# Broadcasting 1/rms over the partitions with a diagonal split into two rounded parts

## What is computed

```python
def layer_norm(x, g, b):
    xf = x.astype(jnp.float32)
    mu = jnp.mean(xf, axis=-1, keepdims=True)
    var = jnp.mean(jnp.square(xf - mu), axis=-1, keepdims=True)
    return ((xf - mu) * lax.rsqrt(var + LN_EPS) * g + b).astype(x.dtype)

def rms_norm_2(x, g):
    xf = x.astype(jnp.float32)
    y = xf * lax.rsqrt(jnp.mean(xf * xf, axis=-1, keepdims=True) + EPS)
    return (y * g.astype(jnp.float32)).astype(x.dtype)
...
    m = rms_norm_2(mem, mem_norm_g)
    for layer in range(DEPTH):
        hn = rms_norm_2(h, mix_norm_g[layer])
        ...
        h = h + memory_cross_attention(rms_norm_2(h, xa_norm_g[layer]), m, ...)
        h = h + conv_ffn(rms_norm_2(h, ffn_norm_g[layer]), ...)
```

## Time and profile before

| | |
|---|---|
| median of 3 runs | 990.91 us (990.75 to 991.11) |
| profiled execution, first to last instruction | 989.2 us |
| VectorE busy | 686.6 us (69%) |
| ScalarE busy | 556.1 us (56%) |
| GpSimd busy | 209.3 us (21%) |
| HBM read | 166.81 MB |

### The profile page before, as it was taken

How to read it: one execution, slowest core, us unless ns; L and a number is a source line. 1 busy time by engine, 2 the same in 40 slices (tenths; PEclk the granted TensorE clock), 3 DMA queues, 4 the chain that set the end, 5 groups by cost and what they waited for, 6 DMA issues and landing times.

```text
span 989.2 us, 16695 instructions
## 1 busy us (share of the span) xinstructions
PE 972.1 (98%) x6532; PEld 879.3 (89%) x6532; DVE 686.6 (69%) x1056; ACT 556.1 (56%) x856; POOL 209.3 (21%) x199
## 2 busy tenths in 40 slices
PE   9999989999999999999999999999999999999997
PEld 8779759989988988798899899999898989989985
DVE  5789785854666687665556779776687665767973
ACT  5556673665765474555355466555445555546662
POOL 0002034300344440012003005221044301202610
PEclk9999999999999999999999999999999999999999
DMA  9634425465334447246414655457546432555441
GB/s 363 241 132 166 175 87 208 162 221 214 128 128 141 174 133 271 108 171 213 150 64 170 213 186 187 181 194 281 186 170 255 163 135 93 198 183 181 172 152 43
DMA packets 24831, 172.93 MB, mean 175 GB/s; under 512 B 2752, under 2 KB 2880, under 8 KB 4416
## 3 DMA queue, kind: packets, MB, share of 16 engines
q1 hardware_dynamic: 23040, 160.66, 45.6%
q10 hardware_dynamic: 1728, 11.40, 3.0%
HBM read 166.81 MB, written 5.24 MB: 174 GB/s over the span
## 4 chain that ended last, share of the span: by engine, by line
PE 93%; DVE 2%; ACT 2%; DMA 1%; issue 1%; POOL 0%; SPq 0%; ACTq 0%; DVEq 0%
PE banks L506 38%; PE banks L594 16%; PE banks L512 14%; PE banks L514 7%; PE banks L504 6%; PE banks L656 4%; PE banks L710 1%; DMA raw<-w 1%; PE banks L761 1%; PE banks L762 1%; DVE work L1725 1%; PE banks L743 1%; PE banks L917 1%; PE banks L834 0%; DVE work L1737 0%
## 5 line engine op out<-in xcount | busy, mean ns | idle before, releaser
L1598 DVE TENSOR_TENSOR wl<-raw,wh 128x1024 fp32r<-128x1024 f32 x300 | 379.7, 1275 | 157.4 <-ACT wh L1090 156.0
L1090 ACT ACTIVATE wh<-raw 128x1024 fp32r<-128x1024 f32 x300 | 313.2, 1054 | 180.6 <-PE banks L506 76.1
L512 PE MATMUL banks<-xx,wh 128*128 128x512 f32 x544 | 192.5, 398 | 0.0
L506 PE MATMUL banks<-xx,wh 128*128 128x256 f32 x1024 | 190.3, 284 | 0.0
L506 PE MATMUL banks<-yy,wh 128*128 128x256 f32 x1024 | 187.8, 285 | 0.1
L506 PEld LDWEIGHTS banks<-xx,wh 128*128 128x128 f32 x1024 | 161.4, 192 | 1.4 <-issue 0.5
L506 PEld LDWEIGHTS banks<-yy,wh 128*128 128x128 f32 x1024 | 160.4, 192 | 0.7 <-issue 0.5
L514 PE MATMUL banks<-xx,wl 128*128 128x256 f32 x544 | 151.8, 279 | 0.0
L506 PE MATMUL banks<-xx,wl 128*128 128x256 f32 x512 | 144.8, 283 | 0.0
L506 PE MATMUL banks<-yy,wl 128*128 128x256 f32 x512 | 138.6, 283 | 0.0
L512 PEld LDWEIGHTS banks<-xx,wh 128*128 128x128 f32 x544 | 102.0, 187 | 22.7
(11 more groups left out here) (221 smaller groups left out, 1449.3 us busy)
## 6 DMA issues: line engine op xcount, KB each, us to landing
raw<-w SPq DMA_DIRECT2D x149, 1024.0 KB, 4.8
m_scratch<-yy ACTq DMA_DIRECT2D x2, 1024.0 KB, 5.9
k_scratch<-kt ACTq DMA_DIRECT2D x2, 1024.0 KB, 8.2
kt<-k_scratch ACTq DMA_DIRECT2D x2, 1024.0 KB, 5.8
yy<-m_scratch ACTq DMA_DIRECT2D x2, 1024.0 KB, 6.0
raw<-w SPq DMA_DIRECT2D x2, 512.0 KB, 5.2
h<-xt SPq DMA_DIRECT2D x2, 512.0 KB, 6.1
v<-memt ACTq DMA_DIRECT2D x1, 1024.0 KB, 7.7
```

What stands on the lines that cost most here:

```text
L506: return pe.matmul(b[:, j, :], weights, o_[:, kk, :], start=k0 + k == 0 and q == 0 and (j == 0 or not both_open), stop=k0 + k == KT * p.de ...
L512: pe.matmul(b[:, j, :], wh[:, slot, j, k * P:k * P + P], operand[:, :, tile0 + k0 + k, :], start=k0 + k == 0, stop=False, skip_group_check ...
L1090: act.activation(wh[:, n % 2, j, :], raw[:, n % RAW_SLOTS, j, :], ACT.Copy).then_inc(hi_ready, 1)
L1598: dve.tensor_tensor(wl[:, n % 2, j, :], raw[:, n % RAW_SLOTS, j, :], wh[:, n % 2, j, :].bitcast(F32), ALU.subtract).then_inc(lo_ready, 1)
```

## The change

The diagonals are written in two parts. The first is the scaled identity in the rounded format, the second the scaled identity in fp32 minus the first, rounded too. TensorE multiplies the rounded ones by the first part and adds the product with the second part in the same bank. The rounded ones are made at the start of ScalarE's queue instead of before `vb0`, with a semaphore of their own, for which each broadcast waits. The sums of the second attention then wait for `tri_r` alone.

```diff
-        diag = sb("diag", [P, 2, P])
+        diag = sb("diag", [P, 2, 2, P], F32R)
...
+        ones_ready = sem("ones_ready")
...
             def bcast(name):
 
                 pe.wait_ge(st_diag, 2 * POW[name] + 2)
-                pe.matmul(bank[5][:, 0:S], ones[:, :], diag[:, :, :].rearrange("p a b -> p (a b)"),
-                          start=True, stop=True).then_inc(bc_full, 1)
+                pe.wait_ge(ones_ready, 1)
+                for q in range(2):
+                    mm = pe.matmul(bank[5][:, 0:S], ones_r[:, :], diag[:, q, :, :].rearrange("p a b -> p (a b)"),
+                                   start=q == 0, stop=q == 1)
+                mm.then_inc(bc_full, 1)
...
                 if a == 0:
-                    pe.wait_ge(tri_ready, 2)
+                    pe.wait_ge(tri_ready, 1)
...
+            act.wait_ge(filled, 1)
+            act.activation(ones_r[:, :], ones[:, :], ACT.Copy).then_inc(ones_ready, 1)
             hi(0)
...
             act.activation(tri_r[:, :], c_("tri"), ACT.Copy).then_inc(tri_ready, 1)
-            act.wait_ge(filled, 1)
-            act.activation(ones_r[:, :], ones[:, :], ACT.Copy).then_inc(tri_ready, 1)
             chunks("vb0", v_copy)
...
             def diagonal(name, src):
 
+                both(*[dve.tensor_scalar(diag[:, 0, t, :], ident, src[:, t:t + 1], None, ALU.mult) for t in range(2)])
                 for t in range(2):
-                    dve.tensor_scalar(diag[:, t, :], ident, src[:, t:t + 1], None, ALU.mult).then_inc(st_diag, 1)
+                    dve.scalar_tensor_tensor(diag[:, 1, t, :], ident, src[:, t:t + 1], diag[:, 0, t, :].bitcast(F32),
+                                             ALU.mult, ALU.subtract).then_inc(st_diag, 1)
```

## The result

The changed kernel takes 993.5 us (median of 11 runs, 993.33 to 993.79), the kernel before 990.92 beside it (11 runs, 990.75 to 992.39): a ratio of 1.0026, with a 95% interval of 1.0018 to 1.0034. It is slower by 2.6 us, where 0.4 less was forecast. Of all the executions behind the numbers from here on, one alone had a lower granted clock (g4_fp32_in_layer_norms: 0.753, 1181.49 us), and its ratio leaves it out.

A forecast was written before the change was run, and what follows sets the result against it. TensorE's own work was taken as the bound (93% of the chain). Mem +0.11, var0 +0.14, var1 +0.47, mix0 -0.19 and the other five -0.95 gave -0.42 us: 990.5 from 990.91, own range 990.0 to 991.2, wider range 989.1 to 992.1.

The forecast's parts named there:

- From xa0 on each norm's stretch 0.19 us shorter: Sign expected in the new trace: from xa0 on, each norm's stretch shortens by the 0.19 us saved at its broadcast.
- the other five 5 x -0.19 = -0.95: Term for xa0, ffn0, mix1, xa1 and ffn1: no wait for the diagonal, so each saves 0.19 us, together -0.95.
- Rival 1: The gain comes whole at all nine broadcasts, waits hidden: nine times 0.19, 989.2 us; chance 0.18.
- Rival 2: Rounded destination slows VectorE's first two scalings, diagonal 0.78 us later instead of 0.65: +0.4, 991.3 us; chance 0.14.
- Rival 3: Each rounded product takes half of the old broadcast's 0.43 us, so the savings vanish: 992.0 us; chance 0.06.
- Rival 4: VectorE's chain is on the path at all nine broadcasts, each passing on 0.65 less 0.19: 995.0 us; chance 0.04.
- Saved slot: On TensorE, the rounded pair takes 0.24 us instead of 0.43 per broadcast: 0.19 saved, 1.7 over nine without waits.
- VectorE's chain: Two more operations and a wait on VectorE make the last diagonal and the next low half 0.65 us later.
- Waits: TensorE waits for the later diagonal 0.30 us at mem, 0.33 at var0, 0.22 at var1, and nowhere else.
- The term of mem: At mem's broadcast, a wait of 0.30 us less the saved 0.19 makes +0.11.
- The stream at var1: Layer norm var1: the stream's scalings start 0.47 us later, and TensorE takes this whole at zf: +0.47 in all.
- The gate: Behind var0, scalings start 0.59 us late, but the gate's first low half keeps 0.10 of room: nothing lost, narrowly.

The follow-up runs named there:

- g4_fp32_in_layer_norms: Changed kernel with the two rounded products one product tile apart at seven norms, the layer norms as in the kernel before; 992.04 us against 991.16, ratio 1.0009.
- e2_tensor_alone: Kernel before, with diagonals written once, rounded, and two rounded products of the same diagonal per broadcast, the second overwriting; 992.31 us against 991.17, ratio 1.0011.
- k2_layer_norms_fp32: Changed kernel with the two layer norms back to one fp32 diagonal and product, rounded pair at the other seven; 993.29 us against 991.30, ratio 1.0020.
- k3_three_parts: k2_layer_norms_fp32 with the low part in two products of 128 columns, so three products in a row; 993.28 us against 991.30, ratio 1.0020.

## Why the prediction was wrong, point by point

**The step that failed** is one that was never written as a term. The sum costs a product by its own slot and by the waits around it, and takes it that all other products keep the time they had: "From xa0 on each norm's stretch 0.19 us shorter", the term "the other five 5 x -0.19 = -0.95", and the same for mix0. The slots did come out of the broadcasts: lateness falls by 0.18 at mix0 and 0.20 at xa0. But the stretches behind them are longer by 6.6 ns a pair, 2.8 us in all. The trace of before had the sign of it: 512-column products of the same line at 236.6 ns in gb and 230.5 to 232 in fu0, fd0 and cc. I read durations of single records around the broadcasts and never compared the pace of two stretches of the same code. A rival "the pairs behind change their pace", priced at the 6.1 ns between gb and fu0 over the some 450 pairs that turned slow (2.7 us), could have been worked out from that alone, though not which way the pace would turn.

**No rival had this mechanism.** Rival 1 (the gain whole) falls with the waits of 0.36, 0.27 and 0.15 us. Rival 2 (the rounded destination slows the scalings) falls with 286 ns. Rival 3 (rounded products no cheaper than half of the old one) falls with 0.23 us for the pair (478.16 to 478.39). Rival 4 had the right sign, but its mechanism, VectorE's chain on the path at all nine, falls too: TensorE waits at three, and with VectorE's part alone the kernel stays at +1.0 us.

**The local terms held.** Saved slot: 0.19 forecast; by lateness 0.18 at mix0 and 0.20 at xa0. VectorE's chain: from the first scaling to the low half 0.65 later than before (353.20 less 0.13, for 352.42), as forecast. Waits: 0.30, 0.33 and 0.22 forecast at mem, var0 and var1, 0.36, 0.27 and 0.15 measured; with the slots taken off, lateness moved by nearly 0 at mem (forecast +0.11), +0.14 at var0 (+0.14) and +0.02 at var1 (+0.03). The term of mem was too high: the weight load had a lead of 0.22 us on its product there (101.15 and 101.37), where a 512-column product stands before it, against 0.12 at var0 (186.60 and 186.72), so part of the load's wait did not reach the products (102.03 before and 102.02 after for the second product behind the broadcast). The stream at var1: 0.48 for 0.47, and it passed to TensorE at the low half of zf whole, lateness +0.61 there, of which 0.15 was there before. The gate was forecast to lose nothing, narrowly, and it loses nothing: 193.74 for the 193.63 of the earlier trace rows is the 0.11 that it brought along.

**Two rules that the prediction named.** The rule of the Trainium skill in "VectorE: DVE Perf Modes" (What auto-detection actually checks), by which an fp32 destination type isn't asked for, now has its number: 286 ns with the rounded destination, as with the fp32 one. That of the Trainium skill in "FP8 and Floating Point Precision" (TensorE Precision Notes) gives four passes for true fp32; taken against one for the rounded format it would give, as an estimate, 4 x 0.12 = 0.48 us for the old broadcast, where the run with the single rounded product shows 0.12 + 2.7 / 9 = 0.42.

**What is shown and what isn't.** Shown: the loss is the slow pace of the apart pairs, 2.8 us; it comes with two rounded products at the broadcasts and not with VectorE's work; the pairs behind are fast with one, three or five equal products in their place from xa0 on, with a two-column product ahead, with an fp32 product behind, or, up to the next wait and in the one execution that was traced, a tile later. Not shown: what sets the pace. The number of products, their format and their order each fail as the only cause, and fd0 shows two paces behind the same instructions at the same distances. So something outside TensorE's own row of instructions, or a state of it that the trace doesn't hold, takes part; no run tells which. Why gb is slow in every kernel is open as well. So is the second half of fd0: it is slow in the changed kernel, e2_tensor_alone and k2_layer_norms_fp32, the three with two equal rounded products alone at the old places, and fast in k3_three_parts, whose broadcasts are followed by the slow pace too.

## What to carry to other kernels

When TensorE bounds the kernel, price an edit by its own slot and then ask what it does to the pace of the long streams behind it: take the start-to-start time of the same kind of product in several stretches of the trace, and if there are two values, their difference times the count of the stream is the size of a rival, of either sign. When a small edit moves the time and no wait has moved, follow the lateness of one engine instruction by instruction against the old trace; a slope means pace, a step means a wait. An edit that falls on the slow side may be cured by a needless product of a few columns or by moving its place, so measure one or two such variants before giving the edit up.

## What the runs showed of the hardware that was not expected

- An alternating stream of 512- and 256-column rounded products runs at 346.7 or 353.3 ns a pair at the same granted clock (0.998). It changed only at a wait or where something other than a pair stood between, was kept through up to a hundred pairs, and behind the broadcasts it was the same at six places in kernels as different as the one before and the one with five products. The slow pace is a rhythm of three pairs (349, 350 and 361 ns in fu0 of the changed kernel).
- At the five norms from xa0 on the pace went with what stood between two such stretches: two equal products slow; one, three, four, five, fp32, or two columns and two fast; 256 + 128 + 128 slow. At mix0 two and four, and two columns and two, were slow, and 256 + 128 + 128 was fast.
- A product of two columns costs 0.03 us there (477.41 to 477.44), and here it was worth 0.5 us behind it in fu0 alone (46.15 us in the changed kernel, 45.60 with it).
- But in fd0 the pace differed (346.9 and 353.4 ns) behind 62 us of the same instructions at the same distances.
- A copy of 1/rms that was finished 0.17 us later (its ScalarE copy at 478.07 for 477.90, g4_fp32_in_layer_norms) cost a new wait of 0.19 us two microseconds on, by way of VectorE's eviction.
